# A decoder trunk on one core: the turning of W1 and conv-input results moves from TensorE to VectorE and POOL's transfers

## The reference

```python
def short_conv_mixer(h, w_in, conv_w, conv_b, w_out):
    b_gate, c_gate, u = jnp.split(h @ w_in, 3, axis=-1)
    gated = c_gate * u
    y = causal_depthwise_conv(gated, conv_w) + conv_b      # width 3
    return (b_gate * y) @ w_out

def sq_relu_mlp(h, w1, b1, w2, b2):
    return jnp.square(jax.nn.relu(h @ w1 + b1)) @ w2 + b2
```

## Time and profile before

| | us |
|---|---|
| timed runs, median of 3 | 2265.49 (2264.67 to 2268.17) |
| span of the profiled execution | 2263.0 |
| TensorE busy | 2228.7 |
| VectorE busy | 1686.1 |
| ScalarE busy | 1180.4 |
| POOL busy | 7.7 |

### The profile page before, as it was taken

The page is one execution under the profiler, slowest core; times in us unless marked ns, Lnnn a source line. Parts: engine busy times, 40 slices in busy tenths (PEclk is TensorE's granted clock), DMA queues, the critical chain, the costliest instruction groups (busy, mean ns, idle before and its releaser), DMA issues.

```text
span 2263.0 us, 28130 instructions
## 1 busy us (share of the span) xinstructions
PE 2228.7 (98%) x10886; PEld 1880.6 (83%) x10886; DVE 1686.1 (75%) x1690; ACT 1180.4 (52%) x1517; POOL 7.7 (0%) x25
## 2 busy tenths in 40 slices
PE   6999999999999999999999999999999999999998
PEld 5999987888888888888888888888888888888886
DVE  7899999986777777778778788878665555555567
ACT  4777784565355345445464444437634544543642
POOL 0000000000000000000000000000000000000000
PEclk9999999999999999999999999999999999999999
DMA  9999998799888888888859778876877667666662
GB/s 353 388 387 397 398 365 310 242 331 326 300 292 277 289 298 284 284 309 273 270 180 371 268 279 306 308 230 218 287 234 235 225 226 241 212 188 189 192 223 103
DMA packets 281525, 627.09 MB, mean 277 GB/s; under 512 B 19233, under 2 KB 27953, under 8 KB 279345
## 3 DMA queue, kind: packets, MB, share of 16 engines
q1 hardware_dynamic: 278432, 608.25, 78.4%
q10 hardware_dynamic: 2960, 17.05, 1.9%
HBM read 623.12 MB, written 2.10 MB: 276 GB/s over the span
## 4 chain that ended last, share of the span: by engine, by line
PE 93%; DVE 4%; issue 1%; DMA 1%; ACT 1%; SPq 0%; DVEq 0%; ACTq 0%
PE bank L1300 27%; PE bank L1302 27%; PE bank L1301 27%; PE bank L1290 3%; PE bank L1293 3%; PE bank L1292 3%; PE bank L1310 2%; DVE mod_acc L910 1%; PE bank L1328 1%; DMA raw<-in_attn_w_qkv 0%; DVE w_low L954 0%; DMA res<-in_x 0%; PE bank L1347 0%; PE bank L1372 0%; PE bank L1360 0%
## 5 line engine op out<-in xcount | busy, mean ns | idle before, releaser
L628 ACT ACTIVATE w_high<-raw 128x1024 fp32r<-128x1024 f32 x752 | 791.4, 1058 | 971.3 <-PE bank L1302 946.2
L954 DVE TENSOR_TENSOR w_low<-raw,w_high 128x1024 fp32r<-128x1024 f32 x752 | 915.8, 1223 | 501.7 <-ACT w_high L628 500.8
L1300 PE MATMUL bank<-w_high,h_high 128*128 128x512 f32 x1632 | 640.1, 392 | 2.9 <-DVE w_low L954 2.9
L1302 PE MATMUL bank<-w_high,h_low 128*128 128x512 f32 x1632 | 635.4, 389 | 0.0
L1301 PE MATMUL bank<-w_low,h_high 128*128 128x512 f32 x1632 | 635.3, 389 | 0.0
L910 DVE SCALAR_TENSOR_TENSOR mod_acc<-mod_raw,cond,mod_acc 128x1024 f32<-128x1024 f32 x345 | 442.1, 1281 | 27.2 <-DMA mod_raw<-in_mod_w 22.8
L1300 PE MATMUL bank<-w_high,hid_high 128*128 128x512 f32 x1120 | 437.2, 390 | 0.0
L1302 PE MATMUL bank<-w_high,hid_low 128*128 128x512 f32 x1120 | 435.8, 389 | 0.0
L1301 PE MATMUL bank<-w_low,hid_high 128*128 128x512 f32 x1120 | 435.8, 389 | 0.0
L1300 PEld LDWEIGHTS bank<-w_high,h_high 128*128 128x128 f32 x1632 | 306.5, 188 | 66.7 <-issue 3.6
L1302 PEld LDWEIGHTS bank<-w_high,h_low 128*128 128x128 f32 x1632 | 306.3, 188 | 64.2
(11 more groups left out here) (151 smaller groups left out, 1165.7 us busy)
## 6 DMA issues: line engine op xcount, KB each, us to landing
raw<-in_mlp_w SPq DMA_DIRECT2D x512, 512.0 KB, 4.5
mod_raw<-in_mod_w SPq DMA_DIRECT2D x368, 512.0 KB, 6.8
raw<-in_attn_w_qkv SPq DMA_DIRECT2D x96, 512.0 KB, 10.6
raw<-in_conv_w_in SPq DMA_DIRECT2D x96, 512.0 KB, 5.5
raw<-in_attn_w_o SPq DMA_DIRECT2D x32, 512.0 KB, 7.2
raw<-in_conv_w_out SPq DMA_DIRECT2D x32, 512.0 KB, 4.7
mod_raw<-in_mod_w SPq DMA_DIRECT2D x32, 256.0 KB, 6.6
gate_row<-in_mod_b ACTq DMA_DIRECT2D x4, 1024.0 KB, 7.5
```

What stands on the lines that cost most here:

```text
L628: act.activation(chunk_slots(n)[0], raw[:, n % NCH], ACT.Copy).then_inc(high_done, 1)
L954: dve.tensor_tensor(low_, raw[:, n % NCH], high.bitcast(F32), ALU.subtract).then_inc(raw_used, 1)
L1300: pe.matmul(dst, high[:, k, c], wh, start=first, stop=False, skip_group_check=True)
L1302: return pe.matmul(dst, low[:, k, c], wh, start=False, stop=last, skip_group_check=True)
```

## The change

A unit is turned in two steps without TensorE. VectorE transposes each 32x32 block out of PSUM into stage[:, 0] (turn_quads). Then blocks must change partitions: POOL issues 16 transfers (swap_quads), each moving 32 partitions x 1 KB from one block of 32 partitions of stage[:, 0] to another of stage[:, 1]. The result has another order within a partition, and feat and by_quads are views that undo it. ScalarE's and VectorE's consumers wait for the count of the transfers (swapped). The consumers' calls move by one chunk: ScalarE's from behind chunk 4 to behind chunk 5 (`late`), VectorE's from behind step 5 to behind step 6. For conv units 4 to 11 ScalarE's copy goes, and VectorE reads the transferred data itself. The group's banks are freed by VectorE's transposes. ScalarE's copy_rows, TensorE's turn and its hooks go.

```diff
-        rows_loop = flat(stage[:, 0]).rearrange("p (t n) -> p t n", t=TT)
+        turned_quads = flat(stage[:, 0]).rearrange("p (c n) -> p c n", c=QUADS)
+        feat_quads = flat(stage[:, 1]).rearrange("p (a n) -> p a n", a=QUADS)
-        feat = stage[:, 1]
+        def by_quads(t):
+            return flat(t).rearrange("p (n a s) -> p n a s", a=QUADS, s=32)
+        feat = flat(stage[:, 1]).rearrange("p (a n s) -> p n a s", a=QUADS, s=32)
+        def feat_of(m):
+            return feat_quads[:, :, m * T // QUADS:(m + 1) * T // QUADS]
...
+            def swap_quads(u):
+                i = u - U_CIN
+                if 0 < i <= NG:
+                    pool.wait_ge(y_copied, i)
+                else:
+                    pool.wait_ge(post_done, CREDIT_STAGE + (u if i <= 0 else u - NG))
+                pool.wait_ge(banks_free, UNIT_GROUPS[u] + BANK0 + CREDIT_BANKS + 1)
+                for a in range(QUADS):
+                    for c in range(QUADS):
+                        pool.dma_start(feat_quads[32 * c:32 * (c + 1), a, :], turned_quads[32 * a:32 * (a + 1), c, :]
+                                      ).then_inc(swapped, 16)
...
-            for n in range(LNS - 1):
-                pool.wait_ge(mod_done, mods_written(block_of(need[n])))
-                coefficients(n)
+            until = [0, U_CIN, U_MLP[1], len(UNIT_GROUPS)]
+            for n in range(LNS):
+                for u in range(until[max(n - 1, 0)], until[n]):
+                    swap_quads(u)
+                if n < LNS - 1:
+                    pool.wait_ge(mod_done, mods_written(block_of(need[n])))
+                    coefficients(n)
...
-                    if late and j == SLOTS:
+                    if late and j == SLOTS + 1:
...
-            def copy_rows(par, dst):
-                act.activation(dst[:, 0, :], bank[2 * par][:, :], ACT.Copy)
-                act.activation(dst[:, 1, :], bank[2 * par + 1][:, :], ACT.Copy).then_inc(rows_done, 1)
...
-                act.wait_ge(rows_turned, f * NG + U_MLP[layer] + g + 1)
-                act.wait_ge(post_done, f * NG + CREDIT_STAGE + S_MLP[layer] + g)
+                act.wait_ge(swapped, SWAP_DMAS * (f * NG + U_MLP[layer] + g + 1))
...
-                    ins = act.activation(feat[:, m, :], bank[2 * (g % 2) + m // 2][:, T * (m % 2):T * (m % 2 + 1)],
-                                         ACT.Relu, bias=vec[:, at:at + 1])
+                    ins = act.activation(feat_of(m), feat_of(m), ACT.Relu, bias=vec[:, at:at + 1])
...
+            def turn_quads(u):
+                w = UNIT_GROUPS[u]
+                if u:
+                    dve.wait_ge(swapped, SWAP_DMAS * u)
+                dve.wait_ge(chunk_mult, w * NCH + CREDIT_SPLIT + NCH)
+                for t in range(TT):
+                    ins = dve.transpose(turned_quads.rearrange("p c (m t s) -> p t m c s", m=GT, t=TT)[:, t],
+                                        bank[2 * (u % 2) + t][:, :].rearrange("p (m c s) -> p m c s", m=GT, c=QUADS))
+                ins.then_inc(banks_free, 1)
...
-                steps(f * (2 * NG) + g + W_MLP[layer], None, late, SLOTS + 1, each, SLOTS if f or g else NCH)
+                steps(f * (2 * NG) + g + W_MLP[layer], None, late, SLOTS + 2, each, SLOTS if f or g else NCH)
+                turn_quads(U_MLP[layer] + f * NG + g)
...
-            def turn(u, par, rows):
-                pe.wait_ge(rows_done, u + 1)
-                for m in range(GT):
-                    for t in range(TT):
-                        at = T * (m % 2) + P * t
-                        ins = pe.transpose(bank[2 * par + m // 2][:, at:at + P], rows[:, t, m * P:(m + 1) * P],
-                                           ident[:])
-                ins.then_inc(rows_turned, 1)
```

More of the change, by code:

```diff
@@ L72, in build_trunk @@
     U_CIN = NG * FC
-    TURN_AFTER = 0
+    UNIT_GROUPS = ([W_MLP[0] + f * 2 * NG + g for f in range(FC) for g in range(NG)]
+                   + [W_CIN + i for i in range(3 * NG)]
+                   + [W_MLP[1] + f * 2 * NG + g for f in range(FC) for g in range(NG)])
+    QUADS = P // 32
+    SWAP_DMAS = 16 * QUADS * QUADS
     QUARTERS = KT // GT
@@ L817, in turned_hidden @@
                     at = f * KT + g * GT + b1 + m
-                    ins = act.activation(feat[:, m, :], bank[2 * (g % 2) + m // 2][:, T * (m % 2):T * (m % 2 + 1)],
-                                         ACT.Relu, bias=vec[:, at:at + 1])
-                ins.then_inc(banks_free, 1)
-                act.wait_ge(banks_free, w + BANK0 + CREDIT_BANKS + 1)
-                act.activation(feat, feat, ACT.Square).then_inc(squared, 1)
+                    ins = act.activation(feat_of(m), feat_of(m), ACT.Relu, bias=vec[:, at:at + 1])
+                ins.then_inc(lifted, 1)
+                act.wait_ge(lifted, f * NG + g + layer * NG * FC + 1)
+                act.activation(stage[:, 1], stage[:, 1], ACT.Square).then_inc(squared, 1)
                 act.wait_ge(squared, f * NG + g + layer * NG * FC + 1)
@@ L825, in turned_hidden @@
                     act.wait_ge(res_done, 2 * TT * HALVES * (2 * layer + 1))
-                act.activation(hid_high[:, g * GT:(g + 1) * GT, :], feat, ACT.Copy).then_inc(hidden_high, 1)
+                act.activation(by_quads(hid_high[:, g * GT:(g + 1) * GT, :]), feat, ACT.Copy).then_inc(hidden_high, 1)
             def mlp(layer):
@@ L843, in turned_conv @@
             def turned_conv(i):
[L844 to L850, removed]
+                act.wait_ge(swapped, SWAP_DMAS * (U_CIN + i + 1))
+                act.activation(by_quads(y[:, i * GT:(i + 1) * GT, :]), feat, ACT.Copy).then_inc(y_copied, 1)
             for i in range(3 * NG):
-                highs(W_CIN + i, (lambda: turned_conv(i - 1)) if i else None, SLOTS if i else NCH)
-                copy_rows(i % 2, rows_loop)
+                highs(W_CIN + i, (lambda: turned_conv(i - 1)) if 0 < i <= NG else None, SLOTS if i else NCH)
                 if i < NG:
                     load_later(1, i)
-            tail(2, lambda: turned_conv(3 * NG - 1))
+            tail(2)
             mlp(1)
@@ L1101, in tail @@
                 for g in range(NG - 1):
-                    steps(w0 + g, None, (lambda: take_both(n, g - 1)) if g else before, SLOTS if g else SLOTS + 1)
+                    steps(w0 + g, None, (lambda: take_both(n, g - 1)) if g else before, SLOTS if g else SLOTS + 2)
                 last = (w0 + NG - 1) * NCH
@@ L1166, in up_group @@
                     each = lambda i: gather(layer, g) if i == 3 else None
-                steps(f * (2 * NG) + g + W_MLP[layer], None, late, SLOTS + 1, each, SLOTS if f or g else NCH)
+                steps(f * (2 * NG) + g + W_MLP[layer], None, late, SLOTS + 2, each, SLOTS if f or g else NCH)
+                turn_quads(U_MLP[layer] + f * NG + g)
             def down_group(layer, f, g):
                 w = f * (2 * NG) + g + W_MLP[layer] + NG
-                steps(w, None, None if g else lambda: turned_hidden(layer, f, NG - 1), SLOTS + 1)
+                steps(w, None, None if g else lambda: turned_hidden(layer, f, NG - 1), SLOTS + 2)
                 dve.wait_ge(y_in, 16 * TT * (layer + 1))
@@ L1207, in turned_conv @@
                     dve.wait_ge(pads, 1)
-                dve.tensor_tensor(gated[:, :, 2:T + 2], feat, y[:, g * GT:(g + 1) * GT, :], ALU.mult
-                                  ).then_inc(conv_step, 1)
+                    dve.wait_ge(y_copied, NG)
+                for m in range(GT):
+                    ins = dve.tensor_tensor(gated[:, m, 2:T + 2].rearrange("p (t a s) -> p t a s", t=TT, a=QUADS),
+                                            feat[:, m * TT:(m + 1) * TT],
+                                            y[:, g * GT + m, :].rearrange("p (t a s) -> p t a s", t=TT, a=QUADS),
+                                            ALU.mult)
+                ins.then_inc(conv_step, 1)
                 steps_ = 1 + 2 * GT
@@ L1229, in _ @@
             for i in range(3 * NG):
-                steps(W_CIN + i, None, (lambda: turned_conv(i - 1)) if i else None, SLOTS + 1,
+                steps(W_CIN + i, None, (lambda: turned_conv(i - 1)) if i else None, SLOTS + 2,
                       (lambda k: residual(1, k)) if i == 1 else None, SLOTS if i else NCH)
+                turn_quads(U_CIN + i)
             tail(2, lambda: turned_conv(3 * NG - 1))
@@ L1416, in chunk, with group @@
                 return ins
-            def group(w, par, high, low, ready=None, hook=None, hook_at=TURN_AFTER):
+            def group(w, par, high, low, ready=None):
                 pe.wait_ge(banks_free, w + BANK0 + 1)
@@ L1424, in group @@
                     chunk(w, par, j, range(TT), high, low).then_inc(chunk_mult, 1)
-                    if hook and j == hook_at:
-                        hook()
                     sum_after(w * NCH + j)
@@ L1499, in o_ready_first, with tail @@
                 o_ready(j)
-            def tail(n, high, low, ready, first_ready, before=None):
```

(3 more changed lines are left out.)

43 lines of the change are left out of this document (18 added, 25 removed).

## The result

The changed kernel takes 2697.96 us (median of 4 runs, 2692.95 to 2699.87) against 2265.95 us for the one before: ratio 1.190, 95% interval 1.1885 to 1.1914, so 432 us slower. The forecast was 2850 us (2460 to 3080), 585 us slower. The profiled execution has a span of 2698.1 us.

The account below looks back on a forecast made before the run. TensorE, busy 2228.7 of 2263.0 us, was taken as the bound: 2263.0 - 38 (transposes gone) + 511 (stalls) + 110 (slow clock) = 2846, with 2.5 for timed runs 2848.5, say 2850 us (range 2460 to 3080).

Parts of the forecast that it names:

- d: POOL's time to issue one transfer, taken as 1.0 us; issues faster than 0.7 us apart would make the prediction wrong.
- Stall = S - 10.35: TensorE's wait before chunk 6 of the group behind an MLP unit: 12.1 us each for 24 units.
- S: Time from a group's end until its turned data is there: 4.3 + 0.2 + 16 d + L, taken as 22.5 us.
- The data's way, 18.2 us: From VectorE's transposes to landed data: POOL's start 0.2, 16 issues of 1.0 and landing 2.0 us.
- L: Landing time of a unit's last transfer, taken as 2.0 us from the quickest landing, 256 KB to the output.
- Rival 1: POOL issues as fast as SP, 0.37 us each: 2304 us; chance 0.16 together with issues of 0.4 to 0.7.
- Stalls 511 us: Sum of TensorE's waits for late turned data in the groups behind the 44 MLP and conv units.
- TensorE's clock 110 us: Slow matmuls on TensorE after each idle time before chunk 6: 44 x 2.5 us.
- TensorE's gain 38 us: 352 transposes removed from TensorE, 8 for each of 44 units: 44 x 0.88 us won.
- VectorE's transposes, two in 1.28 us: Two 128x512 transposes out of PSUM added on VectorE for each unit; 56 us in all, fitting its spare time.
- Rival 2: Transfers hidden, S at most 10.35 us (d = 0.24), no stall and 38 us won: 2227.5 us; chance 0.03.
- Rival 3: POOL's transfers go one at a time, 16 x 2.3 us: 3676 us; chance 0.10 together with d above 1.3.

Follow-up runs that it names:

- experiment 3: Changed kernel without the 704 transfers, VectorE writing its 32x32 blocks straight to where they would land (data not fully turned): 2234.57 us, ratio 0.9857.
- experiment 9: Changed kernel with 35 units consumed at the next group's end, directly ahead of VectorE's next transposes, and 9 turned by TensorE; transfers on POOL: 2297.18 us.
- Experiment 8: Changed kernel with 36 filler matmuls of 512 columns on TensorE before chunk 6 of each group behind a unit: 2687.13 us, ratio 1.185.
- 6: Changed kernel with 16 transfers for each unit carrying half the bytes, 512 B of each partition's 1024: 2666.04 us, ratio 1.1763.
- 7: Changed kernel with 8 whole transfers for each unit in place of 16, the other half not moved: 2528.2 us, ratio 1.1155.
- 1: Changed kernel with `dynamic_dma_scratch_size` 768 in place of 1024: 2727.1 us, ratio 1.203.
- 2: Changed kernel with `dynamic_dma_scratch_size` 1280 in place of 1024: 2687.95 us, ratio 1.186.
- 4: Changed kernel with the same 16 transfers for each unit issued on SP's queue in place of POOL's: 2599.99 us, ratio 1.1464.

## Why the prediction came out as it did

The direction, the place and the mechanism were right: experiment 3 shows that everything lost is the way of the transfers, and the waits lie where the prediction put them, on ScalarE before the Relu and on TensorE before chunk 6. The time, 152 us under the forecast, is partly luck, because the term that the prediction calls decisive is wrong by its own sign: the issues come 0.49 us apart, faster than its 0.7. Put in alone, d = 0.49 takes 44 x 8.2 = 361 us off the forecast and gives some 2490 us; the pauses and the later transposes, which the prediction did not have, made up for more than half of that. By its steps (means of all 44 units of the changed kernel, from the chunk counter and the landings):

- **Stall = S - 10.35: right.** The transposes end 5.2 us after the group's end (4.3 predicted) and the data comes 14.0 us later, so S is 19.2 where the forecast had 22.5. With the measured S of each kind of unit the prediction's list gives 372 us of stalls, and 363 are measured (mean 8.2). In the unit shown above S is 25.8 and the formula gives 15.5; the stall is 13.8, as TensorE too was late and reached chunk 6 only 18.2 us after the group's end, not 16.3. S varies from 14.3 to 25.8, mostly with where VectorE is with its modulation tiles and what it has to work off (the transposes end 3.8 to 11.2 us after the group's end).
- **The data's way, 18.2 us: too long by 4.2.** The prediction had 0.2 + 16 x 1.0 + 2.0. Measured are 0.6 for POOL's start, 16 x 0.49 = 7.8 for the issues, 3.6 for the pauses (5.1 us in 31 of the 44 units) and 2.0 from the last issue's end to its landing, 14.0 in all. So d, taken from POOL's arithmetic, was twice the true one, the term that was mis-sized. L = 2.0, taken from the quickest landing, was right in the mean, though it goes with the loads beside it (1.7 us with none under way, 5.6 beside many in experiment 9) and so with the stall itself. The pause was unforeseen. Rival 1's d of 0.37 was nearer to 0.49, but its time of 2304 us fell to the pauses, the later transposes and the clock.
- **Stalls 511 us: 369 by the waits**, 363 of them in the last two chunks.
- **TensorE's clock 110 us: 104.** The matmuls of the last two chunks of the 44 groups take 346.3 us in place of 242.6, 2.4 for each unit; the one restart counted above loses 5.24 - 2.72 = 2.5. No row ahead of the prediction shows its 2.5 us for a restart: they have the slow stretch of 27 matmuls, not what as many take otherwise. What the runs showed in its place is the 2.4 for each unit, and in the kernel before, behind that stretch of 5.87 us, matmuls of the same size 0.12 us apart (eight steps from 31.87 to 32.83, below), so 27 x 0.12 = 3.24 us and 2.6 lost. Experiment 8 took 76 of the 104 away, and its filler spent 64 elsewhere.

```profile
31.87 0.28 PE L1290 MATMUL bank<-h_high,w_high 128*128 128x256 f32 x1
...
32.83 0.28 PE L1293 MATMUL bank<-h_high,w_low 128*128 128x256 f32 x1
```

- **TensorE's gain 38 us:** 32 in experiment 3, 34 by the chunk counter.
- **VectorE's transposes, two in 1.28 us:** 1.30 for two. Right.
- **Rival 2 (hidden: 2227.5 us)** describes experiment 3, 2234.6 us, and nothing else: with d = 0.49 its condition is far. **Rival 3** is excluded by the issues' distance, 0.49 us.

What the theory of the late data explains in the experiments: the difference in time follows the difference in TensorE's waits, -98 against -97 us (SP), +29 against +27 (768), -10 against -6 (1280), -32 against -31 (half the bytes), -170 against -150 (eight transfers), -142 against -109 (three chunks later). Where the time moves by more than the waits, matmuls at the lower clock are saved with them: the granted clock is 0.956 with eight transfers and 0.948 in the run three chunks later, for 0.927. That the transfers' bytes are what costs is excluded by 6 against 7; that the pauses are the main cause, by 1, 2 and by 4, which has none and still loses 334 us.

## What to carry to other kernels

A way round TensorE is judged by its latency against the work that lies over it, not by the busy time of the engines that it uses: here each engine on the way was under 65% busy, and the kernel lost 19%. If the way is longer than its cover, first move the consumer behind the next group and put the next producer directly behind it, so that no other step lengthens the round, and leave what is needed at once on the old way; that gave back 401 of 432 us, where moving the consumer alone, with steps between it and the next producer, gave 142. Reckon with slower landings once nothing stalls (the last transfer took 5.4 us in experiment 9, 2.5 in the changed kernel), for then the loads run on beside the transfers. Then shorten the way by the number of its transfers (half of them gave 170 us, half their bytes 32), or share them between two queues; with both, and with TensorE still turning the units that are needed at once, the kernel was 0.6% faster than before.

## What was unexpected of the hardware

- POOL issues transfers of 32 partitions 0.49 us apart, SP the same ones 0.63 to 0.67 us apart, though SP issues a 512 KB load in 0.37.
- POOL pauses for about 5 us after 15, 21 or 26 transfers, with a `dynamic_dma_scratch_size` of 768, 1024 or 1280. A pause of 5.1 us delays the data by only 2.5 (14.7 against 12.2 us).
- How soon a transfer of 32 KB lands goes with what else the DMA engines carry. With no load under way POOL's last transfer lands in 1.7 us and SP's in 1.87; beside loads that keep the DMA engines over half busy POOL's takes 5.6 (experiment 9). That the loads are the cause is read from these groups of units; it wasn't tried alone.
